# The last expert chunk of a mixture-of-experts encoder, loaded per half of its columns by one transfer of 32 partitions and twelve of 8

## Chip, cores and metric

The kernel runs on one core of one Trainium2 chip. The metric is the device time of one execution in microseconds (us); with several runs it is their median. A "partition" is one of the 128 rows of the on-chip memory. PE is the matrix engine (PEld its weight loads), DVE the vector engine, ACT the scalar engine, and SP the engine whose queue issues nearly all loads. Sixteen DMA engines move the data of every load.

## What is computed

One hybrid encoder layer on 256 tokens of 1024 features: a mixer in front (gated linear attention beside a long convolution), then 32 experts, four of them chosen per token, then a final RMS norm. The change lies in the experts:

```python
for e in range(N_EXPERTS):
    gu = ht @ w_gate_up[e] + b_gate_up[e]
    gate, up = gu[:, :D_FF], gu[:, D_FF:]
    gate = jnp.minimum(gate, SWIGLU_LIMIT)
    up = jnp.clip(up, -SWIGLU_LIMIT, SWIGLU_LIMIT)
    act = gate * jax.nn.sigmoid(SWIGLU_ALPHA * gate) * (up + 1.0)
    out = out + combine[:, e:e + 1] * (act @ w_down[e] + b_down[e])
```

All weights are float32: 1024 x 2048 for `w_gate_up[e]` and 1024 x 1024 for `w_down[e]`, 12 MB an expert and 384 MB in all.

## The kernel before

**Chunks and slots.** The experts' weights pass through `ring`, 18 slots of 2048 columns by 128 partitions (1 MB each). An expert has 12 chunks of 1 MB: j = 0 to 7 are gate and up weights, j = 8 to 11 are down weights. `CHUNK_ORDER` (lines 141 to 153) is the order in which all 384 chunks are loaded and used; its last eight are the four down chunks of expert 30 and then the four of expert 31. Most transfers take two chunks, the last eight are loaded one by one (`expert_loads`, line 155). Each slot has its own semaphore `moe_loaded`, and `moe_arrival(n)` (line 648) gives the semaphore and count on which a user of chunk n waits.

**SP's queue.** SP issues the loads in that order (line 751), each after a wait on `chunks_used`, the count of chunks that PE has used, which frees the slot. Behind the last but one chunk comes a row of 1024 numbers, the final norm's weights (line 754, one partition), and then the last chunk, n = 383, by two transfers: columns 0 to 1023 and columns 1024 to 2047, each of all 128 partitions with 4 KB in each. The first half counts up the slot's own semaphore, the second `end_loaded`:

```python
            n = E * CH - 1
            sp.wait_ge(chunks_used, n - SLOTS + 1)
            for at, done in ((0, moe_arrival(n)[0]), (D, end_loaded)):
                sp.dma_start(slot((n + MOE_SHIFT) % SLOTS)[:, at:at + D], rows_of(E - 1, CH - 1, 1)[:, at:at + D]).then_inc(done, 16)
```

After that SP reads one number (line 761) and then waits for the output, which it stores (lines 772 and 776).

**PE's order at the end.** Expert 30's gate and up, expert 31's gate and up, expert 30's four down chunks, four matmuls that spread the norm row over the partitions (`spread_norm`, line 1164, after a wait on `norm_loaded`), expert 31's four down chunks, the scatter of expert 30 (line 1127) and of expert 31 (line 1267). `down` (line 1107) takes a chunk in two steps f, one per half of its columns, and each step has two matmuls for the two halves of the output columns, which run beside each other on two halves of the array. The steps on the last chunk are f = 6, behind the wait of `arrived(j)` (line 1199), and f = 7, behind a wait of its own:

```python
            def down(where, arrived, turned=actT, to=2, between=lambda j: None):
                for j in range(GU_CH, CH):
                    arrived(j)
                    for c in range(2):
                        f = 2 * (j - GU_CH) + c
                        if to == 0 and f == DB - 1:
                            pe.wait_ge(end_loaded, 16)
```

Only expert 31's down call has `to == 0`; its matmuls are the rows L1115 with `ring` alone as their input. Behind expert 31's down DVE scales the result in two steps, PE scatters it, ACT takes sums of squares, DVE divides, and SP stores.

Of the kernel before, what the change touches and what calls it, by code (L numbers as in the profile page):

```python
# [15 lines left out]
P = 128  # L16
SEQ = 256
D = 1024
TB = SEQ // P
DB = D // P  # L20
# [9 lines left out]
E = 32  # L30
# [17 lines left out]
SLOTS = 18  # L48
# [5 lines left out]
MOE_SHIFT = 8  # L54
# [5 lines left out]
CH = GU_CH + DN_CH  # L60
# [91 lines left out]
PLACE = {c: n for n, c in enumerate(CHUNK_ORDER)}  # L152


def expert_loads():

    loads, n = [], 0
    while n < E * CH:
        width = 1 if n < 2 * SLOTS or n >= E * CH - 2 * DN_CH else 2
        loads.append((n, width))  # L160
        n += width
    return loads


LOADS = expert_loads()


def expert_arrivals():

    count, arrival = [0] * SLOTS, {}  # L170
    for n, width in LOADS:
        s = (n + MOE_SHIFT) % SLOTS
# [139 lines left out]
def build(nc, ins, out):  # L312
    plan, bank_uses = psum_plan()
    with ExitStack() as ctx:
# [3 lines left out]
        def sem(name):  # L318
            return ctx.enter_context(nc.semaphore(name))
# [237 lines left out]
        sel_first = sem("sel_first")  # L557
        sel_ready = sem("sel_ready")
        moe_loaded = [sem(f"moe_loaded{s}") for s in range(SLOTS)]
        end_loaded = sem("end_loaded")  # L560
        chunks_used = sem("chunks_used")
        gate_ready = sem("gate_ready")
        up_clipped = sem("up_clipped")
# [81 lines left out]
        def slot(s):  # L645
            return ring[:, s * SLOT:(s + 1) * SLOT]

        def moe_arrival(n):

            s, count = ARRIVAL[n]  # L650
            return moe_loaded[s], count

        def gu_banks(e):

            return banks[6:8] if e == 0 else banks[0:2]
# [11 lines left out]
        def _(sp):  # L667
# [19 lines left out]
            def rows_of(e, j, width):  # L687

                if j < GU_CH:
                    r = j // 2 * 2 * P  # L690
                    src = wgu[e, r:r + 2 * P, :].rearrange("(p i) n -> p (i n)", i=2)
                else:
                    r = (j - GU_CH) // 2 * 4 * P
                    src = wdn[e, r:r + 4 * P, :].rearrange("(p i) n -> p (i n)", i=4)
                at = j % 2
                return src[:, at * SLOT:(at + width) * SLOT]
# [53 lines left out]
            sp.dma_start(b_down, ins["b_down"].rearrange("e (h n) -> e h n", h=2)).then_inc(bdown_loaded, 16)  # L750
            for n, width in LOADS[SLOTS:-1]:
                sp.wait_ge(chunks_used, n - SLOTS + width)
                moe(n, width)
            sp.dma_start(normf_row, ins["norm_f_w"].rearrange("(o n) -> o n", o=1)).then_inc(norm_loaded, 16)
            n = E * CH - 1
            sp.wait_ge(chunks_used, n - SLOTS + 1)
            for at, done in ((0, moe_arrival(n)[0]), (D, end_loaded)):
                sp.dma_start(slot((n + MOE_SHIFT) % SLOTS)[:, at:at + D], rows_of(E - 1, CH - 1, 1)[:, at:at + D]).then_inc(done, 16)

            sp.wait_ge(count_ready, 1)  # L760
            longest = sp.value_load(flag[0:1, 0:1], min_val=0, max_val=SEQ)
# [11 lines left out]
            for half in range(2):  # L773
                cs = slice(half * HALF, (half + 1) * HALF)
# [6 lines left out]
        def _(pe):  # L781
# [110 lines left out]
            for stage in STAGES:  # L892
# [9 lines left out]
                elif kind == "filter":  # L902
                    n = f"filter{at[0]}"
# [29 lines left out]
                elif kind == "taps":  # L933
# [3 lines left out]
                    n = f"taps{a}{c}"  # L937
                    begin(n)
                    rows = slice(c // 2 * FFN, (c // 2 + 1) * FFN)
# [32 lines left out]
                elif kind == "updates":  # L972
# [7 lines left out]
                    for k, m, d, n, last_of in ((0, 0, 0, 0, 0), (1, 0, 0, 1, 0), (0, 1, 0, 2, 1), (1, 1, 1, 1, 1), (2, 0, 1, 2, 1), (3, 0, 1, 3, 1)):  # L980
                        if m == 0:
                            begin(f"U{h}{k}")
                        r = (n % 2) * CHUNK
# [4 lines left out]
                elif kind == "output":  # L988
# [7 lines left out]
                    for d, n in ((1, 2), (0, 1), (1, 0), (1, 1), (0, 2), (0, 3)):  # L996
                        r, o = (n % 2) * CHUNK, n // 2 * DV
# [4 lines left out]
                elif kind == "zt":  # L1002
                    a, half = at
# [3 lines left out]
                elif kind == "K":  # L1007
                    ri, half = at
# [5 lines left out]
                elif kind == "Z":  # L1014
                    half, = at
# [17 lines left out]
                elif kind == "mT":  # L1033
                    n, = at
                    pe.wait_ge(merged_ready, TB * (n // 2 + 1))
                    to_feature_major(f"mT{n}", merged, n)
                elif kind == "wo":
                    half, a = at
# [34 lines left out]
                elif kind == "hT":  # L1073
                    a, n = at
# [12 lines left out]
            def half_of(m, k):  # L1087

                return m[:, k % 4, (k // 4) * CAP:(k // 4 + 1) * CAP]
# [17 lines left out]
            def down(where, arrived, turned=actT, to=2, between=lambda j: None):  # L1107
                for j in range(GU_CH, CH):
                    arrived(j)
                    for c in range(2):  # L1110
                        f = 2 * (j - GU_CH) + c
                        if to == 0 and f == DB - 1:
                            pe.wait_ge(end_loaded, 16)
                        for half in range(2):
                            last = pe.matmul(banks[to][half * CAP:(half + 1) * CAP, :], half_of(turned, f),  # L1115
                                             slot(where(j))[:, c * D + half * 512:c * D + (half + 1) * 512],
                                             start=(f == 0), stop=(f == DB - 1))
                    last.then_inc(chunks_used, 1)
                    between(j)
# [44 lines left out]
            def spread_norm():  # L1164

                for half in range(2):
                    pe.matmul(banks[1 + 2 * half], ones[0:1, 0:P], normf_row[:, half * 512:(half + 1) * 512], start=True,
                              stop=True).then_inc(norm_spread, 1)

            def rest_of_gather(j, e):  # L1170

                if j == 1:
                    pe.wait_ge(cslot_ready, e + 1)
                    gather_fill(2, 3, QUAD * CAP)
                elif j == 3:
                    pe.wait_ge(y_ready, e)
                    gather_fill(3, 2, QUAD * CAP)
# [15 lines left out]
            for e in range(E):  # L1193
                g, q = e // QUAD, e % QUAD

                def where(j, e=e):
                    return (PLACE[e, j] + MOE_SHIFT) % SLOTS

                def arrived(j, e=e):
                    pe.wait_ge(*moe_arrival(PLACE[e, j]))  # L1200
                    if j < GU_CH and j % 2 == 0 and e % QUAD == 0:
                        pe.wait_ge([xeT_act, xeT_dve][j // 2 % 2], 2 * (e // QUAD) + 1 + j // 4)

                if e == E - 1:

                    down(lambda j: where(j, E - 2), lambda j: arrived(j, E - 2), between=turn_last)
                    pe.wait_ge(actT_ready, E)
                    pe.wait_ge(norm_loaded, 16)
                    spread_norm()
                    down(where, arrived, actT_last, 0)  # L1210
                    pe.wait_ge(y_ready, E - 1)
                    scatter((E - 2) % 2)
                    continue

                if e == 0:
                    gate_up(q, where, arrived, rest_of_first_gather, to=gu_banks(0))
                else:
                    rest = range(AHEAD if e <= AHEAD_IN else 0, GU_CH)
                    if e == 2:
                        gate_up(q, where, arrived, start_scatters, rest)  # L1220
                    elif q == 0:
                        gate_up(q, where, arrived, lambda j, e=e: rest_of_gather(j, e))
                    else:
                        gate_up(q, where, arrived, chunks=rest)
                    pe.wait_ge(y_ready, e)
                    if e > 1:
                        scatter((e - 1) % 2)
                if 2 <= e <= 5:
                    k = e - 2
                    if k == 0:  # L1230
                        pe.wait_ge(bdown_loaded, 16)
                    pe.matmul(banks[4 + k], combT[:, k // 2 * P:(k // 2 + 1) * P], b_down[:, k % 2, :], start=False, stop=True,
                              skip_group_check=True)
                if q == QUAD - 1 and e < E - 1:
                    pe.wait_ge(cslot_ready, e + 1)
                    pe.wait_ge(sel_ready, g + 2)
                    for k in range(FILLS // 2):
                        gather_fill(k, 3 - k, QUAD * CAP)
                    pe.wait_ge(xeT_act, 2 * g + 3)
                    pe.wait_ge(xeT_dve, 2 * g + 3)  # L1240
                if e == 0:
                    for b in range(2):
                        pe.wait_ge(tile_read[b], bank_uses[b])
                    bias(1)
                elif e < E - 1:
                    pe.wait_ge(up_clipped, e + 1)
                    bias(e + 1)
                if e < AHEAD_IN:
                    gate_up(q + 1, lambda j: where(j, e + 1), lambda j: arrived(j, e + 1), chunks=range(AHEAD))
                pe.wait_ge(cslot_ready, e + 1)  # L1250
                pe.wait_ge(act_ready, e + 1)
                turn_act()
                pe.wait_ge(actT_ready, e + 1)
                if e == 0:
                    emptied(pe, "turned")
                if e == E - 2:
                    spread_rows(E - 1)
                    gate_up(q + 1, lambda j: where(j, E - 1), lambda j: arrived(j, E - 1))
                    continue
                down(where, arrived)  # L1260
                spread_rows(e + 1)
            for part, made in zip(y_parts_last, (y_hi_ready, y_ready)):
                pe.wait_ge(made, E)
                for a in range(TB):
                    for half in range(2):
                        r = slice(half * CAP, (half + 1) * CAP)
# [824 lines left out]
```

## Time and profile before

| what | us |
|---|---|
| runs of the kernel | 1257.38, 1258.83, 2429.36 |
| their median | 1258.83 |
| span of the profiled execution, first to last instruction | 1256.9 |
| PE busy in that span | 1176.8 (94%) |
| mean DMA rate over the span | 362 GB/s |

The profile is of one execution; its own time as a run is not given, only the span, which lies 1.9 us under the median. Times in rows are us from the span's start. The profile cuts the span into 40 slices and shows for each the busy share of an engine in tenths and the DMA rate. The granted clock of PE is 9 tenths or more in every slice. Rows of a timeline are: start, duration, engine, line, operation, output<-input, shapes, count, and in brackets the idle time before and what ended it. "Landing" of a transfer is the time from SP's issue to the last count on its semaphore.

### The profile page before, as it was taken

How to read it: one execution, taken by the hardware profiler on the slowest of the kernel's cores; microseconds unless marked ns; L12 is line 12 of the kernel's file. 1: busy time of each engine (PE TensorE's matmuls, PEld its weight loads, DVE VectorE, ACT ScalarE, POOL GpSimd, SP SyncE). 2: the span in 40 equal slices, each digit the busy share in tenths (PEclk: the TensorE clock that was granted, in tenths of full speed). 3: DMA queues.
4: the chain of work that ended last, by engine and by line, in shares of the span. 5: the costliest groups of instructions: out<-in, count | busy, mean ns of one | idle time of the engine just before them, and what ended most of it. 6: DMA issues, size and time to landing. Idle time of an engine off the chain costs nothing.

```text
span 1256.9 us, 13936 instructions
## 1 busy us (share of the span) xinstructions
PE 1176.8 (94%) x5908; PEld 603.2 (48%) x5908; DVE 431.2 (34%) x744; ACT 270.3 (22%) x408; POOL 0.2 (0%) x4
## 2 busy tenths in 40 slices
PE   7999999999999999999999999998998898889987
PEld 6799968888633333333334333333433333333332
DVE  6588968865421221122122112211211221111212
ACT  6865546454310010000001000000100000000002
POOL 0000000000000000000000000000000000000000
PEclk9999999999999999999999999999999999999999
DMA  9444425598799999999999999999999999999996
GB/s 324 127 143 135 135 68 177 173 380 329 294 416 428 428 426 423 428 426 429 427 429 427 427 430 425 427 428 428 428 428 427 428 429 427 428 428 427 429 424 248
DMA packets 66797, 455.20 MB, mean 362 GB/s; under 512 B 6858, under 2 KB 23531, under 8 KB 39342
## 3 DMA queue, kind: packets, MB, share of 16 engines
q1 hardware_dynamic: 65158, 454.00, 88.4%
q8 instruction: 48, 0.79, 0.3%
q10 hardware_dynamic: 1576, 0.29, 0.1%
q14 instruction: 15, 0.12, 0.0%
HBM read 453.22 MB, written 1.05 MB: 361 GB/s over the span
## 4 chain that ended last, share of the span: by engine, by line
PE 68%; DMA 25%; DVE 4%; ACT 2%; issue 1%; SPq 0%; DVEq 0%; ACTq 0%
PE bank L1097 21%; DMA ring<-in_w_gate_up 21%; PE bank L1115 14%; PE total L826 7%; PE bank L826 5%; PE total L814 4%; PE bank L814 3%; DMA ring<-in_w_down 3%; PE bank L1083 2%; PE bank L865 2%; PE total L1097 1%; PE bank L1104 1%; PE bank L889 1%; ACT xn_area L1544 1%; PE total L1127 1%
## 5 line engine op out<-in xcount | busy, mean ns | idle before, releaser
L1097 PE MATMUL bank<-ring,hy_area 128*64 128x512 f32 x1984 | 441.7, 596 | 21.8 <-DMA ring<-in_w_gate_up 21.8
L1097 PEld LDWEIGHTS bank<-ring,hy_area 128*64 128x64 f32 x1984 | 135.6, 137 | 298.6 <-issue 250.9
L1115 PE MATMUL bank<-ring,xn_area 128*64 128x512 f32 x992 | 220.1, 595 | 20.5 <-ACT xn_area L1544 20.3
L1115 PEld LDWEIGHTS bank<-ring,xn_area 128*64 128x64 f32 x992 | 68.4, 137 | 150.6 <-issue 122.8
L1989 DVE TENSOR_SCALAR qk_area<-bank 128x512 f32<-128x512 f32 x31 | 21.4, 692 | 342.6 <-PE bank L1097 342.6
L2000 DVE SCALAR_TENSOR_TENSOR xn_area_r<-bank,tmp_area,xn_area_r 128x512 fp32r<-128x512 f32 x31 | 23.3, 751 | 307.2 <-ACT xn_area_r L1551 307.2
L1540 ACT ACTIVATE qk_area<-qk_area 128x512 f32<-128x512 f32 x32 | 20.2, 631 | 461.2 <-DVE qk_area L1989 461.2
L1671 DVE TENSOR_TENSOR front_r<-ring,slot_r 128x1024 fp32r<-128x1024 f32 x60 | 73.1, 1221 | 24.7 <-ACT slot_r L1361 24.6
L1361 ACT CAST slot_r<-ring 128x1024 fp32r<-128x1024 f32 x60 | 62.7, 1047 | 43.6 <-PE bank L826 23.2
L1551 ACT ACTIVATE xn_area_r<-bank,tmp_area 128x512 fp32r<-128x512 f32 x31 | 21.3, 687 | 229.1 <-PE bank L1115 211.9
L889 PE MATMUL bank<-tmp_area_r 128*128 128x512 f32 x124 | 36.8, 419 | 13.5 <-issue 8.5
L826 PE MATMUL total<-front_r,slot_r 128*128 128x512 f32 x112 | 44.4, 397 | 0.0
L1127 PE MATMUL total<-xn_area_r 64*128 64x512 f32 x248 | 37.1, 417 | 0.0
L1962 DVE TENSOR_SCALAR hy_area<-bank,colw 128x256 f32<-128x256 f32 x32 | 14.0, 479 | 66.2 <-PE bank L865 66.2
L1083 PE MATMUL bank<-tmp_area,tab 64*128 64x256 f32 x128 | 36.1, 402 | 0.7 <-ACT xn_area L1544 0.7
L1544 ACT COPY xn_area<-bank 128x512 f32<-128x512 f32 x31 | 18.2, 586 | 79.6 <-PE bank L1104 79.6
L889 PEld LDWEIGHTS bank<-tmp_area_r 128*128 128x128 f32 x124 | 20.9, 188 | 29.7 <-DVE qk_area L1990 15.5
L1083 PEld LDWEIGHTS bank<-tmp_area,tab 64*128 64x128 f32 x128 | 21.4, 185 | 27.9 <-issue 25.1
L1127 PEld LDWEIGHTS total<-xn_area_r 64*128 64x128 f32 x248 | 21.0, 184 | 27.8 <-issue 25.1
L826 PE MATMUL bank<-front_r,slot_r 128*128 128x512 f32 x80 | 31.1, 389 | 0.0
L1671 DVE TENSOR_TENSOR front_r<-ring,hi_late_r 128x1024 fp32r<-128x1024 f32 x20 | 24.4, 1222 | 14.2 <-ACT hi_late_r L1361 14.2
L826 PE MATMUL total<-slot_r 128*128 128x512 f32 x72 | 28.8, 399 | 0.0
(394 smaller groups left out, 1276.5 us busy)
## 6 DMA issues: line engine op xcount, KB each, us to landing
ring<-in_w_gate_up SPq DMA_DIRECT2D x116, 2048.0 KB, 35.0
ring<-in_w_down SPq DMA_DIRECT2D x54, 2048.0 KB, 35.8
ring<-in_w_in SPq DMA_DIRECT2D x31, 1024.0 KB, 5.5
ring<-in_w_gate_up SPq DMA_DIRECT2D x24, 1024.0 KB, 8.9
ring<-in_w_down SPq DMA_DIRECT2D x19, 1024.0 KB, 11.8
ring<-in_w_branch_gla SPq DMA_DIRECT2D x4, 1024.0 KB, 5.2
ring<-in_w_branch_hy SPq DMA_DIRECT2D x4, 1024.0 KB, 7.1
ring<-in_w_out SPq DMA_DIRECT2D x4, 1024.0 KB, 6.4
```

The lines of the kernel that those rows point to most:

```text
L814: last = pe.matmul(t[:, 0:SEQ], w[:, d, :], act[:, d, :], start=(m == 0 and d == 0), stop=(m == 2 and d == DB - 1))
L826: last = pe.matmul(bank(f"{kind}{half}{a}")[:, :], act[:, d, a * P:(a + 1) * P], w[:, i, :], start=(u == 0 and i == 0 and m == 0), stop=(u ...
L865: last = pe.matmul(banks[bank_of][:, i * width:(i + 1) * width], src[:, a, d_cols(d)], moving, start=(m == 0 and a == 0), stop=(m == 1 and ...
L889: pe.matmul(gu_banks(e)[bk][:, :], b_pick[e % 2][:, bk * P:(bk + 1) * P], part, start=(m == 0), stop=(m == 1))
L1083: last = pe.matmul(banks[3][:, k * SEQ:(k + 1) * SEQ], ident[0:2 * E, k * E + e:k * E + e + 1].to_broadcast([2 * E, P]), posT_combT, start ...
L1097: last = pe.matmul(to[bk][half * CAP:(half + 1) * CAP, :], xeT[:, j, q, :], slot(where(j))[:, c:c + 512], start=False, stop=(j == GU_CH - ...
L1115: last = pe.matmul(banks[to][half * CAP:(half + 1) * CAP, :], half_of(turned, f), slot(where(j))[:, c * D + half * 512:c * D + (half + 1) ...
L1127: last = pe.matmul(banks[4 + 2 * a + half], selT[r, q, a * P:(a + 1) * P], part[r, :], start=False, stop=True, skip_group_check=True)
L1361: nc.scalar.copy(unit_hi(j), unit_of(j)).then_inc(w_hi_ready, 1)
L1544: nc.scalar.copy(turned.rearrange("p c s -> p (c s)"), banks[3][:, :]).then_inc(actT_ready, 1)
L1671: nc.vector.tensor_tensor(unit_of(j, as_r["front"]), unit_of(j), unit_hi(j).bitcast(F32), ALU.subtract).then_inc(w_parts_ready, 1)
L2000: nc.vector.scalar_tensor_tensor(out=y[1], in0=banks[at][:, :], scalar=cslot[:, column:column + 1], in1=y[0].bitcast(F32), op0=ALU.mult, o ...
```

## The change

Each half of the last chunk is loaded by 13 transfers in place of one: partitions 0 to 31 together, then partitions 32 to 127 by eights. All 13 transfers of a half count up one semaphore, `end_loaded[half]`; PE waits for 16 x 13 on it ahead of the two steps of the last chunk, and no longer waits for the slot's own semaphore there.

```diff
+END_ROWS = [slice(0, 32)] + [slice(r, r + 8) for r in range(32, P, 8)]
...
-        end_loaded = sem("end_loaded")
+        end_loaded = [sem(f"end_loaded{half}") for half in range(2)]
...
-            for at, done in ((0, moe_arrival(n)[0]), (D, end_loaded)):
-                sp.dma_start(slot((n + MOE_SHIFT) % SLOTS)[:, at:at + D], rows_of(E - 1, CH - 1, 1)[:, at:at + D]).then_inc(done, 16)
+            for half in range(2):
+                cs = slice(half * D, (half + 1) * D)
+                for rows in END_ROWS:
+                    sp.dma_start(slot((n + MOE_SHIFT) % SLOTS)[rows, cs], rows_of(E - 1, CH - 1, 1)[rows, cs]).then_inc(end_loaded[half], 16)
...
-                        if to == 0 and f == DB - 1:
-                            pe.wait_ge(end_loaded, 16)
+                        if to == 0 and f >= DB - 2:
+                            pe.wait_ge(end_loaded[f - (DB - 2)], 16 * len(END_ROWS))
...
-                    pe.wait_ge(*moe_arrival(PLACE[e, j]))
+                    if PLACE[e, j] < E * CH - 1:
+                        pe.wait_ge(*moe_arrival(PLACE[e, j]))
```

On SP, at the end of the loads, the queue before was this (`in_w_down` is the down weights in memory, `flag` the number read afterwards):

```order
L704 DMA ring<-in_w_down 128x2048 [waits chunks_used] x7
L754 DMA x<-in_norm_f_w 1x1024
L758 DMA ring<-in_w_down 128x1024 [waits chunks_used]
L758 DMA ring<-in_w_down 128x1024
L761 TENSOR_LOAD flag [waits count_ready]
```

Two transfers stand there. With the change the lines are numbered a few higher, and the queue is this:

```order
L707 DMA ring<-in_w_down 128x2048 [waits chunks_used] x7
L757 DMA x<-in_norm_f_w 1x1024
L763 DMA ring<-in_w_down 32x1024 [waits chunks_used]
L763 DMA ring<-in_w_down 8x1024 x12
L763 DMA ring<-in_w_down 32x1024
L763 DMA ring<-in_w_down 8x1024 x12
L766 TENSOR_LOAD flag [waits count_ready]
```

There are 26 transfers in place of two, in the same place, behind the norm row and ahead of the load of `flag`.

On PE, at expert 31's down (`moe_loaded12` and `moe_loaded13` are the slots of its third and fourth chunk), the order before was this:

```order
L1115 MATMUL bank<-ring 64x512 [waits moe_loaded12]
L1115 MATMUL bank<-ring 64x512 x3
L1115 MATMUL bank<-ring 64x512 [waits moe_loaded13]
L1115 MATMUL bank<-ring 64x512
L1115 MATMUL bank<-ring 64x512 [waits end_loaded]
L1115 MATMUL bank<-ring 64x512
L1127 MATMUL total<-xn_area_r 128x512 [waits y_ready]
```

With the change it is this:

```order
L1120 MATMUL bank<-ring 64x512 [waits moe_loaded12]
L1120 MATMUL bank<-ring 64x512 x3
L1120 MATMUL bank<-ring 64x512 [waits end_loaded0]
L1120 MATMUL bank<-ring 64x512
L1120 MATMUL bank<-ring 64x512 [waits end_loaded1]
L1120 MATMUL bank<-ring 64x512
L1132 MATMUL total<-xn_area_r 128x512 [waits y_ready]
```

The waits stand at the same two matmuls as before; only the semaphores, and what must land for them, are others.

## Rows read from the trace of the kernel before

**Rows 1.** The page, part 2: DMA busy tenths and rate in 40 slices.

```profile
DMA  9444425598799999999999999999999999999996
GB/s 324 127 143 135 135 68 177 173 380 329 294 416 428 428 426 423 428 426 429 427 429 427 427 430 425 427 428 428 428 428 427 428 429 427 428 428 427 429 424 248
```

**Rows 2.** The chain that ended last, from 1196 us on: start, us, what.

```profile
1196.37 39.07 DMA ring<-in_w_down
1235.44 0.04 issue
1235.48 1.94 PE bank L1115 x8
1237.42 1.91 PE bank L1167 x4
1239.33 7.21 PE bank L1115 x32
1246.54 1.13 PE total L1127 x8
...
1252.66 0.66 DVEq L314
```

**Rows 3.** The transfers of line 758 alone: SP's time for each, waits, landing.

```profile
L758 SPq DMA_DIRECT2D ring<-in_w_down x2: 3316/3616/3915, 1216.1 to 1220.1; - x2
...
  PEld bank L1115: 0.9, 2
...
DMA to landing us min/median/max: 25.3/26.6/28.0
```

**Rows 4.** Timeline of PE and its weight loads from 1237 us, expert 31's down.

```profile
1237.35 1.98 PE L1167 MATMUL bank<-x,ones 1*128 1x512 f32 x4
...
1239.26 7.28 PE L1115 MATMUL bank<-ring 128*64 128x512 f32 x32
...
1242.88 0.20 PEld L1115 LDWEIGHTS bank<-ring 128*64 128x64 f32 x4 [0.85 <-DMA ring<-in_w_down]
...
1243.80 0.14 PEld L1115 LDWEIGHTS bank<-ring 128*64 128x64 f32 x2 [0.29 <-issue]
1244.22 0.14 PEld L1115 LDWEIGHTS bank<-ring 128*64 128x64 f32 x2 [0.29 <-DMA ring<-in_w_down]
1244.65 0.14 PEld L1115 LDWEIGHTS bank<-ring 128*64 128x64 f32 x2 [0.29 <-issue]
1245.38 0.28 PEld L1115 LDWEIGHTS bank<-ring 128*64 128x64 f32 x4 [0.58 <-DMA ring<-in_w_down]
```

**Rows 5.** Timeline of PE, the same 32 matmuls of expert 29's down.

```profile
1184.60 7.09 PE L1115 MATMUL bank<-ring,xn_area 128*64 128x512 f32 x32 [0.68 <-ACT xn_area L1544]
```

**Rows 6.** Stretches: length, busy PE, PEld, DVE, ACT, POOL, clock, DMA share, GB/s.

```profile
1200.00:1210.00 10.00, 7.68 (x36) 2.52 (x38) 0.33 (x1) 0.00 (x0) 0.00 (x0) 1.00 1.01 428
...
1236.00:1238.00 2.00, 2.00 (x10) 0.66 (x7) 0.00 (x0) 0.53 (x1) 0.00 (x0) 1.00 0.98 403
1238.00:1240.00 2.00, 2.00 (x8) 0.59 (x8) 0.75 (x1) 0.79 (x3) 0.00 (x0) 1.00 0.72 299
1240.00:1242.00 2.00, 2.00 (x12) 0.69 (x10) 0.00 (x0) 1.81 (x3) 0.00 (x0) 1.00 0.53 219
1242.00:1244.00 2.00, 2.00 (x12) 0.51 (x10) 0.00 (x0) 0.11 (x1) 0.00 (x0) 1.00 0.49 199
1244.00:1246.00 2.00, 2.00 (x12) 0.56 (x8) 0.00 (x0) 0.00 (x0) 0.00 (x0) 1.00 0.09 35
```

**Rows 7.** SP's issues at the end, and the landing of the chunk ahead.

```profile
1215.76 0.29 SPq L754 DMA_DIRECT2D x<-in_norm_f_w  x1
1216.10 7.27 SPq L758 DMA_DIRECT2D ring<-in_w_down  x2
1251.84 0.35 SPq L772 DMA_DIRECT2D out_y<-x  x1
...
L704 SPq DMA_DIRECT2D ring<-in_w_down x2: 4247/7893/11539, 1199.9 to 1211.5; - x2
...
ring<-in_w_down SPq DMA_DIRECT2D x1, 1024.0 KB, 31.4
```

**Rows 8.** The page, part 6: small transfers, count, size, us to landing.

```profile
out_y<-x SPq DMA_DIRECT2D x2, 256.0 KB, 3.0
...
x<-in_b_down SPq DMA_DIRECT2D x1, 128.0 KB, 3.0
```

## Prediction

> **What bounds the kernel now.** I read the page's slices first: from the twelfth on the DMA engines are busy all the time and move 416 to 430 GB/s, and only the last slice falls, to 248 [rows 1]. For nearly the whole expert stage the stream of weights sets the time. Then I read where that ends, in the chain that ended last: it runs on a transfer up to 1235.44 us, and from there it is PE without a gap worth naming (8 matmuls of expert 30's last chunk, the four of the norm row, the 32 of expert 31's down, the scatter) and then the tail of sums, division and store up to 1256.9 [rows 2]. The transfer in that piece is expert 30's last chunk, four chunks ahead of the one that the change touches. So the question is whether the last chunk's arrival holds anything up at all.
>
> The last chunk's own transfers say when it comes: the first half is issued at 1216.10 and takes 28.0 us, so it lands at 1244.1; the second is issued at 1220.05 (3.9 us later) and takes 25.3 us, so it lands at 1245.35 [rows 3]. The weight loads of PE say when it is wanted. In an unhindered row of pairs a load comes every 0.43 us with 0.28 to 0.29 us of idle between them; the load at 1244.22, behind the wait for the first half, has 0.29 as well, so that wait cost nothing. The next pair's load is at 1244.65, the one behind the wait for the second half would have come at 1245.08 and came at 1245.38, 0.30 late [rows 4]. But a weight load runs ahead of its matmul: the matmuls it serves can start only when the pair before has streamed, at 1245.08 + 0.43 = 1245.51, by which time those weights are in. The total bears this out: the 32 matmuls took 7.28 us, against 7.09 for the same 32 with all data long there [rows 4, 5]. That is 0.19 us lost to all arrivals together, and a wait of 0.85 us stands at 1242.88, at the chunk before the last [rows 4], which the change leaves alone.
>
> **What the end of the stream looks like.** The stretches of 2 us show it: the share of busy DMA engines is 0.98 up to 1238, then 0.72, then 0.53 and 0.49 from 1240 to 1244, then 0.09 [rows 6]. A flat half means that eight of the sixteen engines have finished while the other eight still work. The sum from 1236 on is 2 x (0.98 + 0.72 + 0.53 + 0.49 + 0.09) = 5.62 us of all engines. The late eight end at about 1244 + 2 x 0.09 / 0.5 = 1244.4, which is 4.2 us of the 5.62; the early eight share the other 1.4 and end on average at about 1238.9. Spread evenly, all would end near 1241.6.
>
> **The change, part by part.** *Rows per engine.* At 428 GB/s over 16 engines [rows 6] a row of 4 KB takes an engine 4096 / 26.75 = 153 ns. Before, each half gives every engine 8 rows. After, the transfer of 32 partitions gives every engine 2. A transfer of 8 rows of 4 KB can use eight engines at most, one row each; if all twelve use the same eight, those get 14 rows per half and the others 2. That is 6 rows, 0.92 us, per half more on one eight and less on the other, 1.84 us over both.
>
> *Which eight.* No 8-partition transfer is in this trace. The nearest row is the norm's, of one partition, so on one engine: it is issued behind the chunk of 1211.5, which lands 31.4 us later at 1242.9 [rows 7], yet PE works with the norm row at 1237.35 [rows 4], 5.5 us before that chunk is complete. The engine that took it is one of the early ones. I take it that the eight engines of the small transfers are those that this single one belongs to. Then the late eight end at 1244.4 - 1.84 and the last half lands near 1243.5, the first at 1244.1 - 0.92 = 1243.2; the early eight end at 1238.9 + 1.84 = 1240.7 on average. The bounds are this gain of 1.84 us and a loss of as much.
>
> The Trainium skill, "DMA: Bandwidth & Descriptors", section "Why a DMA increments its semaphore by 16 and not by 1", says that a hardware-generated transfer runs on the largest number of engines up to 16 that divides its slowest dimension, and on the lowest-numbered ones. By that rule 32 partitions use all 16 engines, 8 use the first eight, and one the first alone; the norm row agrees as far as one row can, and no run here yet shows the eight.
>
> *Ends of transfers.* Each transfer also ends with a count on its semaphore. The two halves land 1245.35 - 1244.1 = 1.25 us apart [rows 3] on 8 rows of 0.153 us, 1.22; so one end costs an engine about 0.03 us. Twenty-four of them are 0.7 us on the early eight: 1241.4. The upper bound is the 3.0 us to land of the smallest transfers with a figure [rows 8], if nothing overlapped; the lower is nothing. I take 0.03, since it is measured inside this stream. The cover is then some 2.5 us: 1241.4 plus about one microsecond from the last packet to the landing (1244.4 against 1245.35) is 1242.4, and PE wants the halves at 1244.22 and 1245.08.
>
> *SP.* It issues 26 transfers. One issue with nothing in its way takes 0.29 to 0.35 us [rows 7], so 26 take 8 to 9 us; the halves took 3.3 and 3.9 us for 8 rows per engine [rows 3], which is 0.41 to 0.49 us per row, so 28 rows on the busiest engines take 11.5 to 13.7 us. By the latter SP is done at 1216.1 + 13.7 = 1229.8, before the engines reach these rows (full share until 1236 to 1238). The dear bound is 26 x 3.6 = 94 us. I take the row-wise price, because the norm's issue of one row, in the same full queue, took 0.29. Queued behind is only the load of `flag` and the stores, first wanted at 1251.84 [rows 7].
>
> *PE.* The two waits stand where they stood, and the semaphores' counts cost nothing on PE. Nothing ahead of the last chunk moves, because each engine works through its queue in order and the chunk before is ahead of it.
>
> **Sum.** The last chunk lands 0.9 and 1.8 us sooner; PE does not start any matmul sooner, since no matmul on it was late. Against the profiled span: 1256.9 + 0 = 1256.9. The median of the runs lies 1.9 us above the span, so the forecast is the median itself, 1258.8.
>
> **Rivals.** *A, slower: the small transfers go to the late eight.* Place: the same two waits on PE. The first half then lands at 1244.1 + 0.92 + 0.36 = 1245.4, the second at 1245.35 + 1.84 + 0.7 = 1247.9, against 1245.51 for the matmul: 2.4 us later, 1261.2. It decides from the point where the second half lands after 1245.5. For it: nothing shows an 8-row transfer. Against: the norm row came early.
>
> *B, much slower: each transfer has a price of its own, in SP or in the engines.* With 3.6 us an issue, the last is out at 1216.1 + 94 = 1310, lands 3.0 us later at 1313, and PE is 68 us late: 1327. It begins to count when SP is not done by about 1240, 0.9 us an issue. For it: the halves' 3.3 and 3.9. Against: the norm's 0.29 between them.
>
> The Trainium skill, the same page, "Rules for kernel authors", says that under 64 KB one pays mostly overhead and asks for 1 MB or more, and "Anatomy of one DMA" puts the fixed cost at some 2.0 us. A small transfer here is 32 KB; an estimate by that page, paid one behind the other, is 24 x 2.0 = 48 us. The 0.03 us between the halves speaks against its being paid in series.
>
> *C, a little faster: the last chunk's wait does count.* The profile books 0.9 us of PE's idle time before weight loads to these two transfers [rows 3], and at most 0.19 us shows in the matmuls [rows 4, 5]. It would give 1257.9 to 1258.6. For it: the second load was 0.30 us late. Against: the matmuls behind it were not.
>
> *D, the change doesn't do what it says:* the rows of the twelve spread evenly over all sixteen engines. Then landing stays at 1245.35 plus 12 ends of 0.03, 0.4 us, within what the weight load's lead takes: 1258.8 to 1259.1.
>
> **How the numbers follow.** Chances: forecast 0.74, C 0.10, A 0.08, D 0.05, B 0.03. The two neighbouring runs lie 1.45 us apart, so the range goes from the lowest run less C's 0.9 and that spread, 1257.38 - 0.9 - 1.45 = 1255.0, to A's 1261.2 + 1.45 = 1262.7; it leaves out B. A measurement of this kernel tells about 2%, 25 us, from no change. Only B is above that; I give 0.03 to slower, 0.01 to faster for what I have overlooked, and 0.96 to the same.
>
> **What would show it.** Right: the DMA share after 1240 stays above a half for about 2 us and then falls at once; the transfers of 8 partitions land by about 1243.5; the weight load behind `end_loaded1` has 0.29 us of idle before it like its neighbours; the 32 matmuls of expert 31's down still take 7.2 to 7.3 us, with the wait at the chunk before the last as it was; SP's 26 issues end by 1230. Wrong: those 32 matmuls take 8 us or more and the idle time stands at the last chunk (A, or B if SP is still issuing after 1240); or they take under 7.15 us (C).

## The result, and the profile after

The change made the kernel slower: 1262.27 us, the median of 10 runs, beside 1257.34 of the kernel before, the median of 10 runs on the same chip. The ratio is 1.0037 [1.0028, 1.0045], so 4.7 us with an interval of 3.5 to 5.7. (One run of each kernel was far longer, 2429.36 and 4216.87 us; the ratio leaves these two out.) The time lies inside the range, but "no change" was the wrong forecast. It came out near rival A (1261.2), which had 0.08. That nearness is in part luck: A added 2.4 us to a median of 1258.8, measured are 4.7 on 1257.34, and A's mechanism is less than half of it in the profile.

The profiled execution took 1261.46 us, with a span of 1259.7, beside 1256.9 before. The page's part 2 of the kernel after answers to [rows 1]. From the twelfth slice on it stays within 6 GB/s of the one before, except at the very end, where 248 GB/s became 179:

```profile
DMA  9444425598799999999999999999999999999995
GB/s 323 135 137 137 141 71 185 180 387 329 288 422 429 427 429 423 429 426 429 427 428 427 427 428 427 427 428 427 429 427 429 427 429 427 428 427 428 428 424 179
```

PE's timeline of the kernel after, from expert 30's last chunk on (start us, us, what, in brackets the idle time before and what ended it). It answers to [rows 4] and to the PE lines of [rows 2]:

```profile
1232.91 1.94 PE L1120 MATMUL bank<-ring,xn_area 128*64 128x512 f32 x8 [0.39 <-DMA ring<-in_w_down]
1234.78 1.98 PE L1172 MATMUL bank<-x,ones 1*128 1x512 f32 x4
1236.69 1.94 PE L1120 MATMUL bank<-ring 128*64 128x512 f32 x8
1239.98 1.94 PE L1120 MATMUL bank<-ring 128*64 128x512 f32 x8 [1.35 <-DMA ring<-in_w_down]
1243.64 1.94 PE L1120 MATMUL bank<-ring 128*64 128x512 f32 x8 [1.72 <-DMA ring<-in_w_down]
1246.30 1.08 PE L1120 MATMUL bank<-ring 128*64 128x512 f32 x4 [0.72 <-DMA ring<-in_w_down]
1248.86 1.08 PE L1120 MATMUL bank<-ring 128*64 128x512 f32 x4 [1.48 <-DMA ring<-in_w_down]
1249.87 1.20 PE L1132 MATMUL total<-xn_area_r 64*128 64x512 f32 x8
```

Before, the 32 matmuls of expert 31's down stood in one row of 7.28 us. Now they stand in five rows with a wait on a load ahead of the last four, and reach from 1236.69 to 1249.94, 13.25 us. Two of the waits are ahead of chunks that the change does not touch (1239.98 and 1243.64); only the last two are at the halves of the last chunk. The stretches of the same time, which answer to [rows 6] (length, busy PE, PEld, DVE, ACT, POOL, clock, DMA share, GB/s):

```profile
1232.00:1234.00 2.00, 1.61 (x10) 0.48 (x8) 0.00 (x0) 0.00 (x0) 0.00 (x0) 1.00 1.07 383
1234.00:1236.00 2.00, 2.00 (x7) 0.66 (x4) 0.30 (x1) 0.69 (x1) 0.00 (x0) 1.00 0.90 277
1236.00:1238.00 2.00, 2.00 (x8) 0.48 (x8) 0.45 (x1) 1.07 (x2) 0.00 (x0) 1.00 0.93 240
1238.00:1240.00 2.00, 0.65 (x6) 0.02 (x2) 0.00 (x0) 1.49 (x2) 0.00 (x0) 1.00 0.79 223
1240.00:1242.00 2.00, 1.91 (x8) 0.46 (x8) 0.00 (x0) 0.00 (x0) 0.00 (x0) 1.00 0.63 176
1242.00:1244.00 2.00, 0.36 (x2) 0.20 (x4) 0.00 (x0) 0.00 (x0) 0.00 (x0) 1.00 0.32 105
1244.00:1246.00 2.00, 1.57 (x8) 0.29 (x4) 0.00 (x0) 0.00 (x0) 0.00 (x0) 1.00 0.13 51
1246.00:1248.00 2.00, 1.08 (x4) 0.20 (x4) 0.00 (x0) 0.00 (x0) 0.00 (x0) 1.00 0.07 27
```

Read share and rate together, as the rate divided by the share. Before, a share of 0.98 went with 403 GB/s, 411 for a full share; now 0.93 goes with 240, only 258 for a full share. The engines are busy and slow. And at the end there is a tail. Its 51 GB/s are the rate of two engines (428 over sixteen is 26.75 each); in the last stretch the packet records show two engines at work until about 1246.9 and one until 1247.4, which gives the 27.

The issues of SP, which answer to [rows 7], then the rows of line 763 alone, which answer to [rows 3]:

```profile
1213.02 0.29 SPq L757 DMA_DIRECT2D x<-in_norm_f_w  x1
1213.36 19.67 SPq L763 DMA_DIRECT2D ring<-in_w_down  x26
```

```profile
L763 SPq DMA_DIRECT2D ring<-in_w_down x26: 295/559/3912, 1213.4 to 1232.5; - x26
...
  PEld bank L1120: 4.0, 2
  PE bank L1120: 2.2, 2
```

SP is done at 1233.03, 0.76 us an issue. On these transfers the profile books 4.0 us of waiting weight loads and 2.2 us of waiting matmuls, where before it was 0.9 and none. The chain that ended last answers to [rows 2]. Its last transfer is now one of these, where before it was expert 30's last chunk:

```profile
1232.49 16.32 DMA ring<-in_w_down
1248.81 0.04 issue
1248.86 1.10 PE bank L1120 x4
```

**When each chunk is in.** The profile's records of single DMA packets and semaphore counts go one step deeper than its views. Taking the last of the sixteen counts of a chunk (of the halves' counts, the last) as its landing:

```
landing, us               before     after
expert 30's last chunk   1235.44   1232.87
expert 31's first        1237.92   1236.10
expert 31's second       1240.38   1239.93
expert 31's third        1242.84   1243.59
last chunk, half 0       1244.09   1246.26
last chunk, half 1       1245.34   1248.81
```

The two executions are 2.57 us apart at the first of these landings, and as much one chunk earlier (1232.96 and 1230.39). The kernel after is about 2 us ahead at 307 us already, and mostly 2.2 to 3.2 from there on. In the other runs below, the same landing lies between 1232.96 and 1235.83. So the 2.57 belong to the execution and not to the change; I compare from the first of these landings on. The three whole chunks ahead take 10.72 us instead of 7.40, **3.3 us more**, and the last chunk 5.22 instead of 2.50, **2.7 us more**. The 6.0 us together fit PE: from the first matmul on expert 30's last chunk to the first of the scatter it is 16.96 us (1232.91 to 1249.87), against 10.99 before (1235.48 to 1246.47). This figure, "the end stage", is what I use below for single profiles; the medians (4.7 us) weigh the same thing over many executions.

### The profile page after: what moved, and what is told of

Read it like the earlier page. It is cut to its first block, busy times and chain, and to the rows that moved or that the text cites. A ratio compares the mean times of both kernels' runs of the same rounds, so it can differ in the third digit from the quotient of the medians.

```text
span 1259.7 us, 13960 instructions
## 1 busy us (share of the span) xinstructions
PE 1175.6 (93%) x5908; PEld 601.5 (48%) x5908; DVE 431.1 (34%) x744; ACT 269.8 (21%) x408; POOL 0.2 (0%) x4
## 4 chain that ended last, share of the span: by engine, by line
PE 71%; DMA 20%; DVE 4%; ACT 2%; issue 1%; SPq 1%; DVEq 0%; ACTq 0%
PE bank L1102 24%; DMA ring<-in_w_gate_up 18%; PE bank L1120 14%; PE total L831 6%; PE bank L831 5%; PE total L819 4%; PE bank L819 3%; PE bank L870 2%; PE bank L1088 2%; DMA ring<-in_w_down 1%; PE bank L1109 1%; SPq L763 1%; ACT xn_area L1550 1%; PE total L1102 1%; PE bank L894 1%
## 5 line engine op out<-in xcount | busy, mean ns | idle before, releaser
L1109 PE MATMUL bank<-tab,qk_area 128*128 128x128 f32 x128 | 22.2, 296 | 6.6 <-DVE qk_area L2001 6.6
```

The lines of the kernel that those rows point to most:

```text
L1109: last = pe.transpose(banks[3][:, c * P:(c + 1) * P], act[:, c:4 * P:4], ident)
```

## The experiments

The theories at this point:

- **Late engines:** the eight engines of the small transfers are not all early; the chunk's wait ends with the latest of them, which has 14 rows per half instead of 8.
- **Crowding:** transfers of fewer partitions than 128 make DMA engines write at the same places of the on-chip memory, and they slow one another and the chunks ahead. Either because neighbouring partitions are written together, or because each engine has places of its own in a full load and leaves them in a partial one.
- **Smallness:** many small transfers are dear by themselves, or their reading is, wherever they are written.

Four kernels ran on one chip (median of the kernel before: 1257.82), then four on another (1258.09).

**Every fourth partition.** The twelve small transfers per half take partitions 4 apart instead of 8 neighbours:

```diff
-END_ROWS = [slice(0, 32)] + [slice(r, r + 8) for r in range(32, P, 8)]
+END_ROWS = [slice(0, 32)] + [slice(b + o, b + 32, 4) for b in range(32, P, 32) for o in range(4)]
```

> The twelve small transfers take every fourth partition (8 rows spread over 32) in place of 8 neighbours; same count, same rows per transfer. Two theories. L (late engines): of the eight engines that the small transfers use, some are among the late ones, and each of those has 26 transfers at the end where it had 2; neighbours or not does not matter. L alone: the time of the changed kernel, about 4.7 us over before, and the 32 matmuls of expert 31's down again take 13 us from first to last. S (crowding): 8 neighbouring partitions written at once hold each other up and hold up the chunks that are still arriving (after the change the engines are 0.9 busy from 1234 to 1238 but move only 240 to 277 GB/s, where 0.98 moved 403 before); spread, the rate at that share comes back to about 400 and the chunk before the last is on time. S alone: the time of before. Both: the chunk before the last on time, the last half about 2.7 us late, some 2 to 3 us over before.

Measured: 1262.27 us, ratio 1.0036 [1.0024, 1.0047], as the change itself. The crowding is there, from the same point on:

```profile
1234.00:1236.00 2.00, 1.58 (x10) 0.49 (x8) 0.00 (x0) 0.00 (x0) 0.00 (x0) 1.00 0.99 330
1236.00:1238.00 2.00, 2.00 (x6) 0.66 (x4) 0.75 (x1) 0.69 (x1) 0.00 (x0) 1.00 0.97 240
```

Share 0.97 at 240 GB/s. The crowding does not need neighbouring partitions.

**Sixteen rows instead of eight.** Six transfers of 16 neighbouring partitions take the place of the twelve:

```diff
+END_ROWS = [slice(0, 32)] + [slice(r, r + 16) for r in range(32, P, 16)]
```

> 32 neighbouring partitions and then six transfers of 16 neighbours per half, so that every one of the sixteen engines has 8 rows of a half again. L: no engine has more than before, so only 14 ends of transfers in place of 2, 0.05 us each, 0.6 us at most: the time of before within 1 us. S: 16 neighbours crowd as 8 did or worse, the rate at full share falls to 300 GB/s or less while the transfers run, and the kernel is 2 us or more over before.

Measured: 1259.77 us, 1.0015 [1.0007, 1.0024], +1.9 us. PE's timeline:

```profile
1238.85 1.94 PE L1120 MATMUL bank<-ring 128*64 128x512 f32 x8
1241.88 1.94 PE L1120 MATMUL bank<-ring 128*64 128x512 f32 x8 [1.10 <-DMA ring<-in_w_down]
1244.49 3.89 PE L1120 MATMUL bank<-ring 128*64 128x512 f32 x16 [0.67 <-DMA ring<-in_w_down]
```

The waits at the chunks ahead are still there, and those at the last chunk are gone: its 8 matmuls follow the others without a gap. With 16 rows every engine has a row of each transfer (the records show 112 counts for the seven transfers of a half, sixteen each), so no engine has more to carry. What remains, 1.9 us, is the crowding alone. What went, 2.8 us, I put down to the uneven load for the most part; the packets of the chunks ahead were also somewhat faster (472 ns against 531, in the table below).

**Sixteen rows, 8 apart.** Eight transfers per half, each of every eighth partition:

```diff
+END_ROWS = [slice(o, P, 8) for o in range(8)]
```

> Eight transfers of 16 rows per half, every eighth partition: each engine has 8 rows of a half as before, nothing crowds, only the count of transfers is 16 in place of 2. L and S: before, within 0.8 us (14 more ends of 0.05 us per engine). If small transfers cost something of themselves, whatever their shape: 3 us or more over before, and SP's issues past 1230 us of the profile.

Measured: 1260.08 us, 1.0023 [1.0013, 1.0033]. This was meant to avoid the crowding and did not. The nearest of its expectations was the price of small transfers by themselves, 3 us or more. The later runs decide against that one: I had spread the rows of a transfer over the partitions, without asking which engine writes which of them.

**Which eight engines.** The kernel before, with its norm row loaded into 8 partitions (7 of them unused) as a marker for the engines of an 8-partition transfer:

```diff
-            sp.dma_start(normf_row, ins["norm_f_w"].rearrange("(o n) -> o n", o=1)).then_inc(norm_loaded, 16)
+            sp.dma_start(x[0:8, 1, :], ins["norm_f_w"].rearrange("(o n) -> o n", o=1).to_broadcast([8, D])).then_inc(norm_loaded, 16)
```

> The kernel before, with the norm's row loaded into 8 partitions by one transfer of 8 rows in place of one row into one partition; nothing else is changed. It is a marker: its eight landings show which of the sixteen engines, by how late they are on the chunk ahead of it, carry a transfer of 8 rows. Forecast's reading (the eight are the early ones): all eight landings come within 3 to 4 us of the first and before the ninth engine has finished the chunk ahead. L: at least one of the eight lands with the late engines, 5 us or more after the first, and PE's four matmuls on the norm row start that much later. Time: before within 1 us by the former, up to 5 us more by the latter since those matmuls stand ahead of expert 31's down.

Measured: 1266.12 us, one execution. The row brings eight counts, so a load of 8 partitions is moved by eight of the sixteen engines and not by all. These are the sixteen counts of the third chunk of expert 31, which stands ahead of this row in every queue, and the eight of the row:

```
chunk, us after 1233.92:  0 .30 .59 1.02 1.03 1.09 1.51 3.20 | 5.05 6.03 6.19 6.20 6.42 6.47 6.74 7.43
row:   1234.21 1234.70 1235.34 1235.39 1235.75 1237.50 | 1240.56 1240.88
```

Six of the eight engines come within 3.6 us of the chunk's first count, as its eight early ones do, and two at 6.6 and 7.0 us: **two of the eight are late ones.** A wait for all eight ends with them. PE shows it, with the wait at the norm row:

```profile
1241.01 3.75 PE L1167 MATMUL bank<-x,ones 1*128 1x512 f32 x4 [5.10 <-DMA x<-in_norm_f_w]
1244.69 9.31 PE L1115 MATMUL bank<-ring 128*64 128x512 f32 x32
```

The run is 8.3 us over before, where the expectation allowed up to 5. The wait of 5.10 us is within that; the rest is the matmuls themselves, 3.75 and 9.31 us instead of 1.98 and 7.28 (see the last section).

**Written low, written high.** Two counterparts with the same number of transfers, sizes and engines, both as "every fourth partition". In the first, the small transfers of rows 64 to 127 are written to partitions 0 to 63 of an area that is free by then, so all small writes go to partitions 0 to 63; in the second those of rows 32 to 63 go to partitions 64 to 95 there, so all small writes go to 64 to 127. Each kernel leaves out the loading of the rows in question into the slot. The edit of the one and of the other:

```diff
+                    b = rows.start // 32 * 32
+                    if b >= 64:
+                        to = gla_area[slice(rows.start + (-64), rows.start + (-64) + 29, 4), cs]
...
+                    if b == 32:
+                        to = gla_area[slice(rows.start + (32), rows.start + (32) + 29, 4), cs]
```

> As the run with every fourth partition, but the small transfers of rows 64 to 127 are written to partitions 0 to 63 of an area that is no longer used (the last chunk's rows 64 to 127 are therefore not loaded). Source rows, sizes, counts and order stay. Theory P (places): in a load of all 128 partitions each of the sixteen engines writes partitions of its own, and engines that write into the same part share its bandwidth; so the transfers of 8 rows hold up, and are held up by, the engine whose partitions they write. If the eight engines of the small transfers own partitions 0 to 63, these transfers now stay among their own, and the late engines that own 64 to 127 are not held up: the chunk before the last lands nearly on time and the time is 1 to 2.5 us under that of the every-fourth run, that is 2 to 3.5 us over before (what the late ones among the eight cost remains). Theory H (reading): what crowds is on the reading side or in the transfers' small size: nothing changes, 4.5 us over before.

> The counterpart: the small transfers of rows 32 to 63 are written to partitions 64 to 127 of the unused area (the last chunk's rows 32 to 63 are not loaded), so that all small transfers write into partitions 64 to 127. P: all of them now write where other engines write: the rate at full share falls at least as far as in the every-fourth run, and the time is the same as there or up to 2 us more, 4.5 to 6.5 us over before. H: as the every-fourth run, 4.5 us over before, and the same as the run with all writes in 0 to 63.

Measured: written low 1261.32 us, 1.0024 [1.0015, 1.0033]; written high 1264.11, 1.0042 [1.0028, 1.0056]. Stretches of the kernel written low:

```profile
1236.00:1238.00 2.00, 2.00 (x6) 0.57 (x6) 0.75 (x1) 0.79 (x2) 0.00 (x0) 1.00 0.88 338
1238.00:1240.00 2.00, 2.00 (x12) 0.71 (x10) 0.00 (x0) 1.82 (x3) 0.00 (x0) 1.00 0.82 328
```

and of the kernel written high:

```profile
1236.00:1238.00 2.00, 2.00 (x6) 0.66 (x4) 0.75 (x1) 0.69 (x1) 0.00 (x0) 1.00 0.98 225
1238.00:1240.00 2.00, 1.98 (x9) 0.49 (x8) 0.00 (x0) 1.67 (x3) 0.00 (x0) 1.00 0.93 211
1240.00:1242.00 2.00, 0.00 (x0) 0.00 (x0) 0.00 (x0) 0.89 (x2) 0.00 (x0) 1.00 0.86 193
1242.00:1244.00 2.00, 1.44 (x6) 0.48 (x8) 0.00 (x0) 0.00 (x0) 0.00 (x0) 0.93 0.78 180
1244.00:1246.00 2.00, 1.12 (x4) 0.00 (x0) 0.00 (x0) 0.00 (x0) 0.00 (x0) 0.50 0.55 125
```

For a full share that is 384 and 400 GB/s against 230 and 227. Only the place of writing differs, so it is the place that crowds, not the size of the transfers, their number or the reading. Written low, the uneven load remains, nearly bare (the three whole chunks ahead take 8.13 us, 0.7 more than before):

```profile
1241.87 1.94 PE L1125 MATMUL bank<-ring 128*64 128x512 f32 x8 [0.69 <-DMA ring<-in_w_down]
1244.70 1.08 PE L1125 MATMUL bank<-ring 128*64 128x512 f32 x4 [0.89 <-DMA gla_area<-in_w_down]
1247.30 1.08 PE L1125 MATMUL bank<-ring 128*64 128x512 f32 x4 [1.51 <-DMA gla_area<-in_w_down]
```

From the third chunk's landing to half 1's it takes 1247.30 - 1241.87 = 5.43 us, against 2.50 before, 2.9 us more; by the ratio the kernel is 3.0 us slower. In written high PE stood idle from 1240 to 1242, and from 1244 to 1246 its granted clock was 0.50, the lower of the two levels (1.2 GHz). That cost nothing here: its last four matmuls began at 1251.43, 0.04 us behind the last half's landing at 1251.39.

**Split by columns instead.** Each half by four transfers of all 128 partitions and 256 columns, 1 KB per row and 128 KB each:

```diff
+END_ROWS = [0, 1, 2, 3]
...
+                for k in END_ROWS:
+                    part = slice(half * D + k * 256, half * D + (k + 1) * 256)
+                    sp.dma_start(slot((n + MOE_SHIFT) % SLOTS)[:, part], rows_of(E - 1, CH - 1, 1)[:, part]).then_inc(end_loaded[half], 16)
```

> Each half by four transfers of all 128 partitions and 256 columns (1 KB rows, 128 KB a transfer): as many bytes per engine as before, small transfers, but every engine writes its own partitions. P: the time of before within 0.8 us, and the rate at full share stays above 390 GB/s until the early engines end. H, if it is the small size of a transfer: 1.5 us or more over before.

Measured: 1257.62 us, 0.9991 [0.9982, 1.0]. PE:

```profile
1239.15 7.44 PE L1121 MATMUL bank<-ring 128*64 128x512 f32 x32
```

One row again, as in [rows 4]: eight transfers with rows a quarter as long cost nothing. That speaks a second time against smallness, though these transfers are four times as big as the change's small ones.

**Two transfers of 64 partitions** per half, four in all, 256 KB each:

```diff
+END_ROWS = [slice(0, 64), slice(64, P)]
```

> Each half by two transfers of 64 partitions with 4 KB rows: all sixteen engines, 8 rows each, only 2 more ends per engine. P: engines write partitions of others, so the rate at full share falls to 300 GB/s or less while they run, and the time is 1 to 2 us over before, as with the transfers of 16 rows, although there are only four transfers. H or a price per transfer: before within 0.5 us.

Measured: 1260.05 us, 1.0016 [1.0007, 1.0025], +2.0 us, with four big transfers in place of 26.

```profile
1232.00:1234.00 2.00, 2.00 (x11) 0.75 (x11) 0.00 (x0) 0.58 (x1) 0.00 (x0) 1.00 1.06 391
1234.00:1236.00 2.00, 2.00 (x11) 0.61 (x8) 0.00 (x0) 0.06 (x1) 0.00 (x0) 1.00 1.02 246
...
1243.25 3.65 PE L1120 MATMUL bank<-ring 128*64 128x512 f32 x16 [1.45 <-DMA ring<-in_w_down]
```

Full share at 246 GB/s, and the wait stands ahead of the third chunk. Crowding needs no small transfer; loads of half the partitions do it too.

The theory that the place decides had its numbers on record for these four runs: 2 to 3.5 us over before (measured 3.0), 4.5 to 6.5 (5.3), within 0.8 of before (0.5 below by the medians), and 1 to 2 over (2.0).

**All together.** The mean time of one 8 KB packet of the whole chunks between 1237 and 1238 us comes from the packet records. "Three ahead" is the time from the landing of expert 30's last chunk to that of expert 31's third, "last" from there to the landing of the last half. The end stage comes from PE's rows as above (for the split in 64, where PE did not wait for expert 30's last chunk, from its landing; the 17.56 has about 0.5 us of PE's lower clock in it). The last column is the ratio times 1258 us:

| kernel | 8 KB packet, ns | three ahead, us | last, us | end stage, us | slower by, us |
|---|---|---|---|---|---|
| before | 312 | 7.40 | 2.50 | 10.99 | 0 |
| the change | 531 | 10.72 | 5.22 | 16.96 | 4.7 |
| every fourth partition | 539 | 11.14 | 4.87 | 17.56 | 4.5 |
| sixteen rows | 472 | 9.42 | 2.81 | 13.24 | 1.9 |
| sixteen rows, 8 apart | 547 | 10.29 | 3.23 | 14.53 | 2.9 |
| written low | 336 | 8.13 | 5.42 | 14.56 | 3.0 |
| written high | 584 | 12.45 | 4.72 | 18.17 | 5.3 |
| by columns | 314 | 7.42 | 2.72 | 11.14 | -1.1 (-2.3 to 0) |
| two of 64 partitions | 508 | 10.24 | 2.22 | 13.9 | 2.0 |

The two causes separate. Slow packets stretch the three chunks ahead, and an uneven load stretches the last chunk (4.7 to 5.4 us; 2.2 to 3.2 with even engines). With slow packets and even engines the kernel is 1.9 to 2.9 us slower (both kernels of sixteen rows, two of 64), with fast packets and uneven engines about 3 us (written low), with both 4.5 to 5.3. No version beats the kernel before; the split by columns, which has neither, is level with it.

## Why the prediction was wrong

- **What bounds the kernel: right.** PE did not wait for the last chunk, so nothing was to be gained from its coming sooner. The split by columns, which changes only how many transfers there are, shows that: level.
- **"Which eight": wrong.** "I take it that the eight engines of the small transfers are those that this single one belongs to." One engine's early landing was read as that of a group of eight. The marker shows six of the eight early and two late, and the change's own tail is two engines. The sum also went on with the mean of eight engines (1240.7, then 1242.4). Since a landing is the latest of its engines, two are enough: the late ones got the 6 rows more per half that the prediction worked out, and the last chunk took 5.22 us instead of 2.50. Rival A's terms for this, 1.84 us for rows and 0.7 for ends, make 2.54; measured were 2.7 in the kernel after and 2.9 written low. The size was right, the side was wrong, and "late eight or early eight" was the wrong question: a mixed eight, which it was, stood in no rival.
- **"Nothing ahead of the last chunk moves, because each engine works through its queue in order": wrong.** Nothing here speaks against the order within an engine, but the early engines start on the small rows while the late ones still have up to three chunks to write. From there on packets of the chunks ahead take longer, 531 ns instead of 312 between 1237 and 1238. This was the dearer part in the profile, 3.3 of 6.0 us, and 1.9 to 2.9 us by the ratios of the three kernels with crowding alone. No rival had it.
- **The row's price, "153 ns":** right as long as each engine writes in its own place (the packet records give 159 for 4 KB), wrong by up to about a factor of two where it does not.
- **"Ends of transfers", 0.03 us each: right.** At the very end one engine finishes small transfers at 1248.42, 1248.62 and 1248.81, 0.195 us apart, with packets of 0.159: 0.036 an end. (The Trainium skill, "DMA: Bandwidth & Descriptors", section "Anatomy of one DMA", gives the 2.0 us that the prediction quotes for transfers issued by GpSimd; these are issued by SP.)
- **SP: right in effect.** Done at 1233.03, forecast 1229.8. It took 19.67 us against 13.7: 0.70 us for each of the 28 rows, above the row-wise 0.41 to 0.49, and 0.76 an issue, under the 0.9 from which B would have begun. By columns SP needed 22.8 us for 8 issues, and nothing was late.

**The place of writing.** The pair written low and high shows that the place decides. With the kernels of 16 and 64 rows it fits one reading: in a load of 128 partitions each engine writes partitions that no other engine writes, and engines at one place share its rate. No record of these runs says which engine writes where. Packets take up to about twice their time: in "every fourth partition" the longest between 1236 and 1241 are 328 ns for 4 KB and 634 for 8 KB, where the kernel before has 159 and 309 at least. Single packets took longer (480 ns for 4 KB in written low).

The Trainium skill, "DMA: Bandwidth & Descriptors", section "The descriptor swizzle", gives the partitions: in a 128-partition load engine 0 writes partitions 0 to 3 and 32 to 35, engine 1 the next four of each, up to engine 7, and engines 8 to 15 do the same from 64 on. The Trainium skill, "SBUF — State Buffer", section "Door 1: The DMA port swizzle (why `[64,N]` ≈ `[32,N]`)", says that these eight partitions share one of 16 ports. By that, rows 4 apart of partitions 0 to 63 put each of the first eight engines on its own port (written low: 336 ns, agrees), of partitions 64 to 127 on a port of the other eight (written high: 584 ns, agrees), and two transfers of 64 put two engines on each (508 ns, agrees). Rows 8 apart put two engines on one port too, by which that run had to miss. Four engines of a transfer of 8 neighbours would share a port by this rule, and yet few packets took more than about twice their time (the longest 4 KB packet of the change took 396 ns); that they are seldom there at once is my guess, and it was not tried. The prediction had used the rule on how many engines a transfer gets, from the first of these two pages, and had not asked where they write.

The Trainium skill, "DMA: Bandwidth & Descriptors", section "Rules for kernel authors", advises against two transfers to disjoint partition halves, since both use the same engines. The run with two of 64 agrees with the advice. But sharing the engines is not what cost 2.0 us here: the pieces by columns share them as well and cost nothing.

## What to carry to other kernels

Split a load by columns and keep all 128 partitions in each piece: four pieces per half cost nothing here, while two pieces per half by partitions cost 2.0 us, and slowed loads ahead of them in the queue. A load lands when its latest engine does, so one that runs on some of the engines, with more for each, is late as soon as one of them is behind. And before a load is made to come sooner, look whether its user waits for it: here PE did not, so there was only something to lose.

## What was not expected of the hardware

**The engines drift apart by 7 us in one stream.** All sixteen carry the same bytes, yet the third chunk of expert 31 is finished over a span of 7.3 us (before, us after the first engine, by the semaphore's counts; then the same after the change):

```
before:  0 .35 .63 1.18 1.29 1.38 2.24 3.27 | 6.08 6.16 6.62 6.63 6.90 7.06 7.19 7.31
after:   0 .28 .72 1.67 2.07 2.42 3.55 6.12 | 6.87 8.95 9.36 9.59 9.72 9.78 10.13 10.52
```

I take this drift to be what makes both losses possible, though no run had its engines in step: such engines would not meet on one another's places while whole chunks are still to be written, and none would be late. It builds up in jumps of about 1.5 us of one engine at a time. The page's list of queues has a candidate:

```profile
q8 instruction: 48, 0.79, 0.3%
```

These are packets of 16 KB that fetch instructions, with a median of 1.07 us. The packet records tie the drift to them. In the kernel before, 23 of them fall between 580 us and the end of the stream, and at each of the 23, on the chunks then in flight, one engine's lag grows by 1.4 to 1.7 us. That makes about 35 of the 38 us by which the sum of all lags grows in this time (26 to 64 us); beside the last of the 23, of 1.09 us, one packet of the stream took 0.80 us in place of 0.31, and 1.09 + 0.49 is 1.58. That the fetches cause the jumps is argued from this match; no run left them out.

**An idle PE loses its clock late in the kernel.** In the marker run PE had nothing to do from 1235.9 to 1241.0, and the granted clock fell to 0.50:

```profile
1238.00:1240.00 2.00, 0.00 (x0) 0.00 (x0) 0.00 (x0) 0.00 (x0) 0.00 (x0) 0.74 0.55 227
1240.00:1242.00 2.00, 0.99 (x2) 0.50 (x3) 0.00 (x0) 0.00 (x0) 0.00 (x0) 0.50 0.46 188
```

It stayed there up to 1248. The four matmuls on the norm row took 3.75 us instead of 1.98 and the 32 behind them 9.31 instead of 7.28, with all their weights landed in time: 3.8 us on top of the wait. A late load can so cost more than its lateness.
